# Expert output sums with 640 gathered and 1408 dense columns in place of 576 and 1472, and another place for the wait of a gathered sum

## The chip, the core and the metric

The kernel runs on one core of one Trainium2 chip. The metric is the device time of one execution in microseconds, the median of several. TensorE (PE) multiplies, VectorE (DVE) and ScalarE (ACT) work on tiles, GpSimd (POOL) issues the gathers here and SyncE (SP) issues the plain loads.

## What is computed

One decoder layer on 256 tokens of width 2048: a projection, two groups of recurrent heads, an output projection, and then a layer of 16384 single-neuron experts, with a final norm. The change touches only the second product of the expert layer. Cut to that:

```python
def peer_ffn(h, wq, keys, u_tab, v_tab):      # u_tab, v_tab: (16384, 2048)
    ...                                       # 128 experts and gates for each token
        u = jnp.take(u_tab, eb, axis=0)
        act = jax.nn.gelu(jnp.einsum("cd,ced->ce", xb, u))
        vv = jnp.take(v_tab, eb, axis=0)
        return jnp.einsum("ce,ced->cd", gb * act, vv)
...
x = x + peer_ffn(rms_norm(x, norm2_g), ...)
return rms_norm(x, normf_g)
```

## The kernel before

The work goes in stages: input projection with the recurrent heads, output projection, queries and top-16 choice, the product with all of `peer_u` (its result for all 16384 experts lies in `Zq`), a stage of gates (about 1355 to 1486 us of the profile) that turns `Zq` into a matrix of weights, token by expert, that is zero for experts not chosen, and then the V stage (1486 to 1993 us), which multiplies these weights with `peer_v`, and a tail with the final norm (to 2005 us).

**Two ways for V.** The 2048 columns of the output are split at `DD`. The first `DD` = 1472 columns are made densely on PE: for each of 128 expert rows i (a row is a block of 128 experts) SP loads `vraw` (128 partitions by 1472 columns, f32), ACT rounds it to `vhi`, DVE takes the rest as `vlo`, and PE adds three products (`vhi` with `a_hi`, `vlo` with `a_hi`, `vhi` with `a_lo`) into PSUM banks for both halves t of the tokens. The last `DS` = 576 columns are made sparsely: for each token half and each of its 128 picks POOL issues an indirect DMA that gathers one row piece per token into `got`, and DVE adds `got` times a weight to `sums`. That is 256 gathers and 256 sums, two for each expert row.

**Pieces.** Each expert row is loaded, rounded and subtracted in two pieces, k = 2i and 2i + 1: 1024 columns (two chunks of 512 for PE) and 448 columns (one chunk). `V_CUTS` holds the chunk limits; `dense` (L2257 and on) issues 2 x 3 x 3 = 18 matmuls for an expert row, 12 with 512 columns and 6 with 448. For the last expert row all 9 matmuls of t = 0 come before those of t = 1.

**What sets the order.** All queues are written out by hand. SP: `load_v(k)` (L494) waits until PE has finished piece k - 8 (4 buffers `vraw`), then issues the load. ACT: `v_hi(k)` (L948) waits for the load and for PE's piece k - 6 (3 buffers `vhi`). DVE: `v_lo(k)` (L1573) waits for ACT; behind each `v_lo(k)` from k = 6 on stands one `picked` (L1642), at every 40th piece two; every eighth piece has an `act_lo` too (L1634), which prepares the weights of four expert rows. PE: `dense` waits for `v_lo` of its piece. POOL: `gather(k)` (L628) waits until the sum k - 6 is done (6 buffers `got`); between gathers k = 128 and 223 it also issues eight loads of `xr` and four of `gf`.

A sum reads what the sum before it wrote (`sums[:, t]`), so it must not start until that one has landed. Before, `mark` does this: it puts an increment on the sum and a wait for it right behind it:

```python
def mark(ins, name, value):
    ins.then_inc(sem(name), 1)
    dve.wait_ge(sem(name), value)
```

so the wait holds whatever comes next on DVE, which mostly is a `v_lo`. The tail adds the dense sums to `xr` (L1675), squares, scales and sends rows out.

In the stage of gates, SP also issues the first eight pieces of `vraw` (one at every sixth step, from L522 on) between the small loads `oneJ` and `oneI` that PE and POOL need there.

Of the kernel before, what the change touches and what calls it, by code (L numbers as in the profile page):

```python
# [84 lines left out]
U_EXP = 50  # L85
U_FIRST = 65

DD = 1472
DS = D - DD
N_V_COLS = (PIECE, DD - PIECE)  # L90
V_CUTS = (0, 512, 1024, DD, D)
TOK4 = 4
LAST_TOKENS = (slice(0, 64), slice(64, SEQ))
N_TOK4 = SEQ // TOK4
# [3 lines left out]
N_GATHER = 6  # L98
V_RAWS, V_HIS = 4, 3
# [73 lines left out]
def hybrid_layer_kernel(nc, a, out):  # L173
    ctx = ExitStack()
    with ctx:
        sems = {}

        def sem(name):
            if name not in sems:
                sems[name] = ctx.enter_context(nc.semaphore(name))  # L180
            return sems[name]
# [4 lines left out]
        def at(name, shape, dt, offset):  # L186
            return nc.alloc_sbuf_tensor_at(name, shape, dt, offset=offset)
# [8 lines left out]
        raw_at = base[0]  # L196
# [19 lines left out]
        end = ARENA + 4 * ARENA_F  # L216
# [106 lines left out]
        wgt = at("wgt", [P, SEQ], F32, mshift_at + 1024)  # L323
        vraw = [at(f"vraw{i}", [P, DD], F32, raw_at + 4 * DD * i) for i in range(V_RAWS)]
        vlo = [at(f"vlo{i}", [P, DD], F32R, raw_at + 4 * DD * i) for i in range(V_RAWS)]
        vhi = [at(f"vhi{i}", [P, DD], F32R, raw_at + 24576 + 4 * DD * ((i + 2) % V_HIS))
               for i in range(V_HIS)]
        oneJ = [at(f"oneJ{i}", [P, TOK4, P], F32, raw_at + 43008 + 2048 * i) for i in range(N_ONEJ)]
        oneG = [at(f"oneG{i}", [P, TOK4, P], F32, raw_at + o)
                for i, o in enumerate((51200, 53248, 69632, 71680))]  # L330
# [6 lines left out]
                   for i in range(N_FIRST)]  # L337
        jcast = [at(f"jcast{i}", [P, BC_TOK, P], BF16,
                    raw_at + 4096 * (NR + slots[i // 2]) + 2048 * (i % 2)) for i in range(N_CAST)]
        a_hi = [at(f"a_hi{i}", [P, 4, SEQ], F32R, raw_at + 43008 + 4096 * i) for i in range(2)]  # L340
        a_lo = [at(f"a_lo{i}", [P, 4, SEQ], F32R, raw_at + 51200 + 4096 * i) for i in range(2)]
        got = [at(f"got{i}", [P, DS], F32, raw_at + 59392 + 4 * DS * ((i + 3) % N_GATHER))
               for i in range(N_GATHER)]
        wT = at("wT", [P, NT2, PICKS], F32, raw_at + 4 * DD * V_RAWS)
        assert 4 * DD * V_RAWS + 1024 <= 24576 and 24576 + 4 * DD * V_HIS <= 43008
        assert 59392 + 4 * DS * 3 >= 65536 + 768 and 59392 + 4 * DS * N_GATHER <= 73728
        madeJ = [ar(f"madeJ{i}", 30720 + 512 * i, [P, TOK4, P]) for i in range(3)]
        madeI = [ar(f"madeI{i}", 32256 + 256 * i, [P, TOK4, P], BF16) for i in range(2)]
        sums = ar("sums", 0, [P, NT2, DS])
        xr = ar("xr", 2048, [P, NT2, DD])  # L350
        gf = ar("gf", 6144, [P, D])
        xr_sq = ar("xr_sq", 8192, [P, 8, DS])
        xg = ar("xg", 13312, [P, PIECE])

        ps = ctx.enter_context(nc.psum_tensor("ps", [P, 8, 512], F32))
        jrow_dram = nc.dram_tensor("jrow_spill", (SEQ, PICKS), BF16, kind="Internal").ap()
# [106 lines left out]
        def _(sync):  # L463
            xv = a["x"].rearrange("o (t p) d -> p (o t) d", p=P)
            for t in range(NT2):
                for q in range(2):
                    part = slice(PIECE * q, PIECE * q + PIECE)
# [26 lines left out]
            def load_v(k):  # L494

                i, half = k // 2, k % 2
                cols_v = slice(PIECE * half, PIECE * half + N_V_COLS[half])
                sync.wait_ge(mm_done, 2 * T_V + max(k - 2 * V_RAWS + 1, 0))
                sync.dma_start(vraw[i % V_RAWS][:, cols_v], a["peer_v"][i, :, cols_v]).then_inc(
                    sem(f"v_in{k % (2 * V_RAWS)}"), 16)  # L500
# [40 lines left out]
            for k in range(2 * V_RAWS, 2 * N_V):  # L541
                load_v(k)
            outv = out.rearrange("o (t p) d -> p (o t) d", p=P)
            for q in range(6):
                t, j = q // 3, (3, 0, 2)[q % 3]
                if t and j == 0:
                    sync.wait_ge(sem("xg_done"), 1)
                else:
                    sync.wait_ge(sem(f"y_done{t}"), 2 if t and j == 2 else q % 3 + 1)
                first, end = V_CUTS[j], D if j == 3 else V_CUTS[j + 1] + (512 if j == 0 else 0)  # L550
                src = sums[:, t] if j == 3 else xg[:, :] if t and j == 0 else xr[:, t, first:end]
                sync.dma_start(outv[:, t, first:end], src).then_inc(sem("out_sent"), 16)
            sync.wait_ge(sem("out_sent"), 96)
# [113 lines left out]
        def _(act):  # L667
# [280 lines left out]
            def v_hi(k):  # L948

                i, half = k // 2, k % 2  # L950
                cols_v = slice(PIECE * half, PIECE * half + N_V_COLS[half])
                act.wait_ge(sem(f"v_in{k % (2 * V_RAWS)}"), 16 * (k // (2 * V_RAWS) + 1))
                act.wait_ge(mm_done, 2 * T_V + max(k - 2 * V_HIS + 1, 0))
                nc.scalar.activation(vhi[i % V_HIS][:, cols_v], vraw[i % V_RAWS][:, cols_v],  # L954
                                     ACT.Copy).then_inc(hi_done, 1)
# [102 lines left out]
        def _(dve):  # L1058
# [28 lines left out]
            def stt(o, i0, s, i1, op0, op1):  # L1087
                return V.scalar_tensor_tensor(out=o, in0=i0, scalar=s, in1=i1, op0=op0, op1=op1)  # L1088
# [126 lines left out]
            for g in range(GROUPS):  # L1215
# [96 lines left out]
                for c in range(4):  # L1312
# [302 lines left out]
            for s in range(N_TOK4 + S_LAG):  # L1615
# [678 lines left out]
```

## Time and profile before

| | us |
|---|---|
| median of 3 runs | 2005.94 (2005.63 to 2006.31) |
| the profiled execution, its own time | 2006.88 |
| its span, first to last instruction | 2005.0 |
| mean granted TensorE clock, share of full speed | 0.995 |
| DVE busy over the span | 1531.8 |
| ACT busy over the span | 975.6 |
| POOL busy over the span | 499.3 |
| HBM read and written | 430.24 MB and 29.43 MB |

The profiled execution took 1.9 us more than its span, and 0.94 us more than the median. PE here is the time in which matmuls are under way, PEld that of weight loads, which overlap it. The DMA share of a window is the mean busy share of the core's 16 DMA engines in it. A row of a timeline gives the start, the time it took, and in brackets how long the engine was idle before and what ended that; records of one kind that follow closely are merged (x2, x8), and the start of the next row is then the better measure of how long they took in the stream.

### The profile page before, as it was taken

To read this page: it belongs to the slowest core of one execution; us is meant where nothing else is said; L and a number is where in the kernel's file an instruction comes from. 1 tells how busy PE (TensorE), PEld (TensorE's weight loads), DVE (VectorE), ACT (ScalarE), POOL (GpSimd) and SP (SyncE) were. 2 spreads that over 40 slices of the span, in tenths; PEclk is the share of its full clock that TensorE was granted. 3 is DMA by queue.
4 is the path that set the end of the run, shared out by engine and by line. 5 is a ranking of instruction groups with operands and counts; after the bars stand their busy time and mean duration, and the time that the engine had idled before them with its cause. 6 is when DMAs were issued, how large, how long until landed. Compare 5 with 4: busy or idle time off the path is not lost.

```text
span 2005.0 us, 36029 instructions
## 1 busy us (share of the span) xinstructions
PE 1949.5 (97%) x14368; PEld 1732.9 (86%) x14368; DVE 1531.8 (76%) x2339; ACT 975.6 (49%) x1394; POOL 499.3 (25%) x511
## 2 busy tenths in 40 slices
PE   8999999999999999999999999999999999999997
PEld 7989888887899888888888888888888888888886
DVE  5557575667535999977878888758879989999997
ACT  5535454464544444444444444446665444444444
POOL 0000000000000000000012222105667666666663
PEclk9999999999999999999999999999999999999999
DMA  7523233245655666666578888768879999999996
GB/s 242 178 87 124 93 109 97 79 157 175 213 173 171 183 187 188 187 183 188 189 249 284 286 285 284 250 190 272 294 231 350 350 338 352 345 349 369 358 349 229
DMA packets 149607, 462.06 MB, mean 230 GB/s; under 512 B 19936, under 2 KB 45056, under 8 KB 148928
## 3 DMA queue, kind: packets, MB, share of 16 engines
q1 hardware_dynamic: 115760, 339.49, 52.3%
q0 software_dynamic: 33680, 120.26, 16.9%
q8 instruction: 115, 1.88, 0.4%
q14 instruction: 52, 0.43, 0.1%
HBM read 430.24 MB, written 29.43 MB: 229 GB/s over the span
## 4 chain that ended last, share of the span: by engine, by line
PE 87%; DVE 5%; DMA 3%; ACT 3%; issue 1%; SPq 0%; DVEq 0%; ACTq 0%
PE ps L1716 86%; DMA oneJ<-oneJ_spill 2%; DVE lo L1080 1%; DMA raw<-in_w_in 1%; ACT hi L677 1%; DMA raw<-in_w_out 0%; DVE hT L1088 0%; DVE xc L1088 0%; DVE TmTT L1292 0%; DVE L L1275 0%; DVE lr L1387 0%; PE ps L1876 0%; ACT x_sq L892 0%; DMA x_sb<-in_x 0%; ACT la L869 0%
## 5 line engine op out<-in xcount | busy, mean ns | idle before, releaser
L1716 PE MATMUL ps<-hT,hi 128*128 128x512 f32 (+1 forms) x3936 | 1075.1, 345 | 8.7 <-DVE rkv L1088 4.9
L1716 PE MATMUL ps<-hT,lo 128*128 128x256 f32 x2992 | 839.7, 281 | 0.0
L1716 PEld LDWEIGHTS ps<-hT,hi 128*128 128x128 f32 x3936 | 680.5, 190 | 108.6 <-DVE rkv L1088 6.0
L1080 DVE TENSOR_TENSOR lo<-raw,hi 128x1024 fp32r<-128x1024 f32 x406 | 492.6, 1224 | 227.7 <-ACT hi L677 221.4
L677 ACT ACTIVATE hi<-raw 128x1024 fp32r<-128x1024 f32 x406 | 424.4, 1059 | 441.0 <-DMA raw<-in_peer_u 371.8
L1716 PEld LDWEIGHTS ps<-hT,lo 128*128 128x128 f32 x2992 | 568.2, 190 | 0.0
L635 POOL DMA_INDIRECT got<-in_peer_v,row_ids x256 | 328.3, 1282 | 159.7 <-DVE sums L1088 98.6
L954 ACT ACTIVATE vhi<-vraw 128x1024 fp32r<-128x1024 f32 (+1 forms) x256 | 202.3, 816 | 271.0 <-DMA vraw<-in_peer_v 264.0
L1578 DVE TENSOR_TENSOR vlo<-vraw,vhi 128x1024 fp32r<-128x1024 f32 (+1 forms) x256 | 237.5, 929 | 43.0 <-ACT vhi L954 21.7
L1716 PE MATMUL ps<-vhi,a_hi 128*128 128x512 f32 (+1 forms) x768 | 251.7, 382 | 1.8 <-DVE a_lo L1634 1.6
L1716 PE MATMUL ps<-vlo,a_hi 128*128 128x512 f32 (+1 forms) x768 | 252.5, 383 | 0.0
L1716 PE MATMUL ps<-vhi,a_lo 128*128 128x512 f32 (+1 forms) x768 | 250.4, 381 | 0.0
L1088 DVE SCALAR_TENSOR_TENSOR sums<-got,wT,sums 128x576 f32<-128x576 f32 x256 | 207.7, 811 | 0.3
L1716 PEld LDWEIGHTS ps<-vlo,a_hi 128*128 128x128 f32 x768 | 144.2, 188 | 28.2
L1716 PEld LDWEIGHTS ps<-vhi,a_lo 128*128 128x128 f32 x768 | 144.2, 188 | 24.6
L1716 PEld LDWEIGHTS ps<-vhi,a_hi 128*128 128x128 f32 x768 | 144.1, 188 | 22.9 <-issue 2.3
L593 POOL DMA_DIRECT2D jrow_spill<-jrow x2 | 1.1, 543 | 452.4 <-DVE jrow L1512 452.4
L580 POOL DMA_DIRECT2D x<-in_x x1 | 0.7, 729 | 374.1 <-DVE yR_lo L1358 374.1
L597 POOL DMA_DIRECT2D oneJ_spill<-madeJ x64 | 34.6, 540 | 205.5 <-DVE madeJ L1554 205.5
L1425 DVE TENSOR_TENSOR Zq<-ps,Zq 128x256 f32<-128x256 f32 x129 | 78.6, 610 | 5.1 <-ACT Zq L922 5.1
L922 ACT ACTIVATE Zq<-ps 128x256 f32<-128x256 f32 x129 | 79.1, 613 | 5.1 <-PE ps L1716 4.8
L1716 PE MATMUL ps<-oneG,oneJ 128*128 128x128 f32 x512 | 69.0, 279 | 7.6 <-DMA oneJ<-oneJ_spill 7.4
(288 smaller groups left out, 1791.6 us busy)
## 6 DMA issues: line engine op xcount, KB each, us to landing
raw<-in_peer_u SPq DMA_DIRECT2D x256, 512.0 KB, 4.3
vraw<-in_peer_v SPq DMA_DIRECT2D x128, 512.0 KB
raw<-in_w_in SPq DMA_DIRECT2D x86, 512.0 KB, 3.6
vraw<-in_peer_v SPq DMA_DIRECT2D x128, 224.0 KB
raw<-in_w_out SPq DMA_DIRECT2D x32, 512.0 KB, 3.6
raw<-in_wq SPq DMA_DIRECT2D x32, 512.0 KB, 3.5
oneJ_spill<-madeJ POOLq DMA_DIRECT2D x64, 256.0 KB, 5.1
oneJ<-oneJ_spill SPq DMA_DIRECT2D x64, 256.0 KB, 4.7
```

The costliest lines, as they stand in the source:

```text
L580: pool.dma_start(x2[:, :, :], a["x"].rearrange("o (t p) d -> p (o t) d", p=P)).then_inc(sem("x2_in"), 16)
L593: pool.dma_start(jrow_dram[t * P:(t + 1) * P], jrow[:, t]).then_inc(sem("jrow_out"), 16)
L597: pool.dma_start(oneJ_dram[g], madeJ[g % 3][:, :, :].rearrange("p t j -> p (t j)")).then_inc(sem(f"oneJ_out{g % 3}"), 16)
L635: pool.indirect_dma_start(out=got[k % N_GATHER][:, :], out_offset=None, in_=v_rows, in_offset=bass.IndirectOffsetOnAxis(ap=row_ids[:, t, e ...
L677: nc.scalar.activation(hi[n % NR][:, :], raw[n % NR][:, :], ACT.Copy).then_inc(hi_done, 1)
L922: nc.scalar.activation(Zq[:, i // 4, part, i % 4], bank("tile", T_U + i)[:, part], ACT.Copy).then_inc(sem("z_in"), 1)
L954: nc.scalar.activation(vhi[i % V_HIS][:, cols_v], vraw[i % V_RAWS][:, cols_v], ACT.Copy).then_inc(hi_done, 1)
L1080: V.tensor_tensor(lo[n % NR][:, :], raw[n % NR][:, :], hi[n % NR][:, :].bitcast(F32), ALU.subtract).then_inc(lo_done, 1)
L1088: return V.scalar_tensor_tensor(out=o, in0=i0, scalar=s, in1=i1, op0=op0, op1=op1)
L1425: V.tensor_tensor(Zq[:, i // 4, part, i % 4], bank("tile", T_U + i)[:, lo_part], Zq[:, i // 4, part, i % 4], ALU.add).then_inc(freed("tile ...
L1578: V.tensor_tensor(vlo[i % V_RAWS][:, cols_v], vraw[i % V_RAWS][:, cols_v], vhi[i % V_HIS][:, cols_v].bitcast(F32), ALU.subtract).then_inc( ...
L1716: return nc.tensor.matmul(o, lhsT, rhs, start=start, stop=stop, skip_group_check=True)
```

## The change

Three things, in one edit:

- `DD` goes from 1472 to 1408, so 64 columns pass from the dense way to the gathered one: a gather moves 640 columns of a row (2560 B) instead of 576 (2304 B), and a sum works on 640. The counts stay at 256 each.
- The dense chunks become 480, 480 and 448 columns (`V_CUTS`), and the first piece of an expert row 960 columns instead of 1024 (`V_PIECE`); the second keeps 448. Offsets of `a_hi`, `a_lo` and `got` move with the sizes, and the parts of the tail that went by 512 and 1024 go by the cuts.
- `picked` no longer waits behind its sum. The wait for the sum before stands in front of the next sum.

```diff
-DD = 1472
+DD = 1408
 DS = D - DD
-N_V_COLS = (PIECE, DD - PIECE)
-V_CUTS = (0, 512, 1024, DD, D)
+V_CUTS = (0, 480, 960, DD, D)
+V_PIECE = V_CUTS[2]
+N_V_COLS = (V_PIECE, DD - V_PIECE)
...
-        a_hi = [at(f"a_hi{i}", [P, 4, SEQ], F32R, raw_at + 43008 + 4096 * i) for i in range(2)]
-        a_lo = [at(f"a_lo{i}", [P, 4, SEQ], F32R, raw_at + 51200 + 4096 * i) for i in range(2)]
-        got = [at(f"got{i}", [P, DS], F32, raw_at + 59392 + 4 * DS * ((i + 3) % N_GATHER))
+        a_hi = [at(f"a_hi{i}", [P, 4, SEQ], F32R, raw_at + 41984 + 4096 * i) for i in range(2)]
+        a_lo = [at(f"a_lo{i}", [P, 4, SEQ], F32R, raw_at + 50176 + 4096 * i) for i in range(2)]
+        got = [at(f"got{i}", [P, DS], F32, raw_at + 58368 + 4 * DS * ((i + 3) % N_GATHER))
...
-                cols_v = slice(PIECE * half, PIECE * half + N_V_COLS[half])
+                cols_v = slice(V_PIECE * half, V_PIECE * half + N_V_COLS[half])
...
             for j in range(2):
-                part = slice(512 * j, 512 * j + 512)
+                part = slice(V_CUTS[j], V_CUTS[j + 1])
...
                 t, e = k // PICKS, k % PICKS
                 dve.wait_ge(sem(f"got_in{k % N_GATHER}"), 16 * (k // N_GATHER + 1))
-                mark(stt(sums[:, t], got[k % N_GATHER][:, :], wT[:, t, e:e + 1], sums[:, t], ALU.mult,
-                         ALU.add), "picks_used", k + 1)
+                if k:
+                    dve.wait_ge(sem("picks_used"), k)
+                stt(sums[:, t], got[k % N_GATHER][:, :], wT[:, t, e:e + 1], sums[:, t], ALU.mult,
+                    ALU.add).then_inc(sem("picks_used"), 1)
...
-            scaled_out(0, xr[:, 0, 0:PIECE], slice(0, PIECE))
+            scaled_out(0, xr[:, 0, 0:V_PIECE], slice(0, V_PIECE))
```

The `cols_v` line changes alike in `load_v`, `v_hi` and `v_lo`, the `part` line in the tail of ACT and of DVE.

No instruction changes its place in a queue; a wait does, and sizes do. On DVE, in the middle of the V stage, the queue stood so before, with the semaphores that each instruction waits for in brackets (`picks_used` counts finished sums, `hi_done` pieces that ACT has rounded, `got_in` landed gathers):

```order
L1088 SCALAR_TENSOR_TENSOR sums<-got_206,wT,sums 128x576 [waits got_in4]
L1578 TENSOR_TENSOR vlo_161<-vraw_157,vhi_165 128x1024 [waits hi_done,picks_used]
L1088 SCALAR_TENSOR_TENSOR sums<-got_207,wT,sums 128x576 [waits got_in5]
L1578 TENSOR_TENSOR vlo_161<-vraw_157,vhi_165 128x448 [waits hi_done,picks_used]
L1634 TENSOR_TENSOR a_lo_201<-Zq,a_hi_199 128x1024 [waits ahi_done]
L1088 SCALAR_TENSOR_TENSOR sums<-got_202,wT,sums 128x576 [waits got_in0]
L1578 TENSOR_TENSOR vlo_162<-vraw_158,vhi_163 128x1024 [waits hi_done,picks_used]
L1088 SCALAR_TENSOR_TENSOR sums<-got_203,wT,sums 128x576 [waits got_in1]
```

and now:

```order
L1089 SCALAR_TENSOR_TENSOR sums<-got_206,wT,sums 128x640 [waits picks_used,got_in4]
L1579 TENSOR_TENSOR vlo_161<-vraw_157,vhi_165 128x960 [waits hi_done]
L1089 SCALAR_TENSOR_TENSOR sums<-got_207,wT,sums 128x640 [waits picks_used,got_in5]
L1579 TENSOR_TENSOR vlo_161<-vraw_157,vhi_165 128x448 [waits hi_done]
L1635 TENSOR_TENSOR a_lo_201<-Zq,a_hi_199 128x1024 [waits ahi_done]
L1089 SCALAR_TENSOR_TENSOR sums<-got_202,wT,sums 128x640 [waits picks_used,got_in0]
L1579 TENSOR_TENSOR vlo_162<-vraw_158,vhi_163 128x960 [waits hi_done]
L1089 SCALAR_TENSOR_TENSOR sums<-got_203,wT,sums 128x640 [waits picks_used,got_in1]
```

The wait for `picks_used` has gone from the `vlo` behind each sum to the next sum, which has a `vlo`, or the `a_lo`, between it and the sum it waits for.

The only place where two sums follow each other is the one at every 40th piece; before, on DVE:

```order
L1578 TENSOR_TENSOR vlo_161<-vraw_157,vhi_164 128x448 [waits hi_done,picks_used]
L1634 TENSOR_TENSOR a_lo_200<-Zq,a_hi_198 128x1024 [waits ahi_done]
L1088 SCALAR_TENSOR_TENSOR sums<-got_205,wT,sums 128x576 [waits got_in3]
L1088 SCALAR_TENSOR_TENSOR sums<-got_206,wT,sums 128x576 [waits got_in4,picks_used]
L1578 TENSOR_TENSOR vlo_162<-vraw_158,vhi_165 128x1024 [waits hi_done,picks_used]
```

and now:

```order
L1579 TENSOR_TENSOR vlo_161<-vraw_157,vhi_164 128x448 [waits hi_done]
L1635 TENSOR_TENSOR a_lo_200<-Zq,a_hi_198 128x1024 [waits ahi_done]
L1089 SCALAR_TENSOR_TENSOR sums<-got_205,wT,sums 128x640 [waits picks_used,got_in3]
L1089 SCALAR_TENSOR_TENSOR sums<-got_206,wT,sums 128x640 [waits picks_used,got_in4]
L1579 TENSOR_TENSOR vlo_162<-vraw_158,vhi_165 128x960 [waits hi_done]
```

There the second sum waits for the first in both, and the `vlo` behind it no longer does.

On PE an expert row (both token halves) stood so before, `x2` being two chunks in a row:

```order
L1716 MATMUL ps<-vhi_163,a_hi_198 128x512 x2
L1716 MATMUL ps<-vlo_159,a_hi_198 128x512 x2
L1716 MATMUL ps<-vhi_163,a_lo_200 128x512 x2
L1716 MATMUL ps<-vhi_163,a_hi_198 128x512 x2
L1716 MATMUL ps<-vlo_159,a_hi_198 128x512 x2
L1716 MATMUL ps<-vhi_163,a_lo_200 128x512 x2
L1716 MATMUL ps<-vhi_163,a_hi_198 128x448
L1716 MATMUL ps<-vlo_159,a_hi_198 128x448
L1716 MATMUL ps<-vhi_163,a_lo_200 128x448
L1716 MATMUL ps<-vhi_163,a_hi_198 128x448
L1716 MATMUL ps<-vlo_159,a_hi_198 128x448
L1716 MATMUL ps<-vhi_163,a_lo_200 128x448
```

and now:

```order
L1719 MATMUL ps<-vhi_163,a_hi_198 128x480 x2
L1719 MATMUL ps<-vlo_159,a_hi_198 128x480 x2
L1719 MATMUL ps<-vhi_163,a_lo_200 128x480 x2
L1719 MATMUL ps<-vhi_163,a_hi_198 128x480 x2
L1719 MATMUL ps<-vlo_159,a_hi_198 128x480 x2
L1719 MATMUL ps<-vhi_163,a_lo_200 128x480 x2
L1719 MATMUL ps<-vhi_163,a_hi_198 128x448
L1719 MATMUL ps<-vlo_159,a_hi_198 128x448
L1719 MATMUL ps<-vhi_163,a_lo_200 128x448
L1719 MATMUL ps<-vhi_163,a_hi_198 128x448
L1719 MATMUL ps<-vlo_159,a_hi_198 128x448
L1719 MATMUL ps<-vhi_163,a_lo_200 128x448
```

The twelve matmuls of 512 columns have 480 now, the order is the same.

## Rows read from the trace of the kernel before

**Rows 1.** The page: busy us of the engines; GB/s in 40 slices.
```profile
PE 1949.5 (97%) x14368; PEld 1732.9 (86%) x14368; DVE 1531.8 (76%) x2339; ACT 975.6 (49%) x1394; POOL 499.3 (25%) x511
...
GB/s 242 178 87 124 93 109 97 79 157 175 213 173 171 183 187 188 187 183 188 189 249 284 286 285 284 250 190 272 294 231 350 350 338 352 345 349 369 358 349 229
```

**Rows 2.** Chain of waits from 1300 us on: start us, us, what.
```profile
1498.75 492.47 PE ps L1716 x2241
...
1991.35 0.70 DVE xr L1675
```

**Rows 3.** Waits, 1500 to 1991 us: who <- whom, us in all, times, longest.
```profile
ACT vhi L954 <- DMA vraw<-in_peer_v: 256.5, 159, 4.7
POOL got L635 <- DVE sums L1088: 98.6, 64, 5.1
...
DVE vlo L1578 <- ACT vhi L954: 21.7, 33, 1.5
```

**Rows 4.** Waits of the SP queue, 1500 to 1991 us.
```profile
SPq L499 <- PE ps L1716: 356.7, 215, 2.8
```

**Rows 5.** Timeline of PE, one expert row: start us, us, what.
```profile
1700.47 0.62 PE L1716 MATMUL ps<-vhi,a_hi 128*128 128x512 f32 x2
...
1703.21 0.36 PE L1716 MATMUL ps<-vhi,a_hi 128*128 128x448 f32 x1
...
1704.42 0.62 PE L1716 MATMUL ps<-vhi,a_hi 128*128 128x512 f32 x2
```

**Rows 6.** Timeline of DVE, the same stretch.
```profile
1699.55 1.23 DVE L1578 TENSOR_TENSOR vlo<-vraw,vhi 128x1024 fp32r<-128x1024 f32 x1
1700.69 0.81 DVE L1088 SCALAR_TENSOR_TENSOR sums<-got,wT,sums 128x576 f32<-128x576 f32 x1
1701.54 0.62 DVE L1578 TENSOR_TENSOR vlo<-vraw,vhi 128x448 fp32r<-128x448 f32 x1
1702.08 0.81 DVE L1088 SCALAR_TENSOR_TENSOR sums<-got,wT,sums 128x576 f32<-128x576 f32 x1
```

**Rows 7.** Timeline of DVE, the tail: two sums with no wait between them.
```profile
1995.38 0.82 DVE L1088 SCALAR_TENSOR_TENSOR sums<-sums,scal,gf 128x576 f32<-128x576 f32 x1
1996.12 1.28 DVE L1088 SCALAR_TENSOR_TENSOR xr<-xr,scal,gf 128x1024 f32<-128x1024 f32 x1
```

**Rows 8.** Groups, 1500 to 1991 us: instructions, count, busy us, mean ns, idle before.
```profile
L635 POOL DMA_INDIRECT got<-in_peer_v,row_ids x250 | 320.2, 1281 | 156.7 <-DVE sums L1088 98.6 <-issue 58.1
...
L1634 DVE TENSOR_TENSOR a_lo<-Zq,a_hi 128x1024 fp32r<-128x1024 f32 x30 | 36.5, 1218 | 0.0
```

**Rows 9.** DMA view, 1495 to 1984 us: packets and bytes.
```profile
DMA packets 56811, 171.00 MB, mean 350 GB/s; under 512 B 8213, under 2 KB 24085, under 8 KB 56779
```

**Rows 10.** Windows: busy us by engine, granted clock, DMA share, GB/s.
```profile
1495.00:1535.00 40.00, 39.87 (x182) 33.79 (x181) 36.80 (x44) 17.63 (x22) 27.59 (x20) 1.00 0.99 354
...
1738.00:1778.00 40.00, 40.00 (x184) 34.19 (x183) 36.95 (x44) 18.79 (x24) 26.93 (x23) 1.00 1.00 369
1834.00:1874.00 40.00, 40.00 (x184) 34.23 (x183) 38.22 (x46) 19.40 (x24) 30.12 (x25) 1.00 1.00 368
1495.00:1984.00 489.00, 488.87 (x2226) 417.57 (x2225) 449.18 (x532) 223.43 (x277) 327.38 (x262) 1.00 0.97 350
```

**Rows 11.** Timeline of all engines, the end of the weight stream.
```profile
1983.20 1.67 ACT L954 ACTIVATE vhi<-vraw 128x1024 fp32r<-128x1024 f32 x2 [2.00 <-DMA vraw<-in_peer_v]
...
1986.35 0.62 DVE L1578 TENSOR_TENSOR vlo<-vraw,vhi 128x448 fp32r<-128x448 f32 x1
...
1989.06 0.83 PE L1716 MATMUL ps<-vhi,a_hi 128*128 128x512 f32 x3
```

**Rows 12.** Timeline of PE in the stage of gates.
```profile
1448.38 1.06 PE L1716 MATMUL ps<-Zq,oneJT 128*128 128x128 f32 x8
1451.97 2.08 PE L1716 MATMUL ps<-oneG,oneJ 128*128 128x128 f32 x8 [2.53 <-DMA oneJ<-oneJ_spill]
```

**Rows 13.** Windows in the stage of gates (columns as rows 10).
```profile
1451.90:1456.00 4.10, 4.03 (x21) 4.03 (x22) 2.02 (x4) 1.07 (x3) 2.04 (x2) 0.58 0.73 267
```

More of the change, by code:

```diff
@@ L339, in hybrid_layer_kernel @@
                     raw_at + 4096 * (NR + slots[i // 2]) + 2048 * (i % 2)) for i in range(N_CAST)]
-        a_hi = [at(f"a_hi{i}", [P, 4, SEQ], F32R, raw_at + 43008 + 4096 * i) for i in range(2)]
-        a_lo = [at(f"a_lo{i}", [P, 4, SEQ], F32R, raw_at + 51200 + 4096 * i) for i in range(2)]
-        got = [at(f"got{i}", [P, DS], F32, raw_at + 59392 + 4 * DS * ((i + 3) % N_GATHER))
+        a_hi = [at(f"a_hi{i}", [P, 4, SEQ], F32R, raw_at + 41984 + 4096 * i) for i in range(2)]
+        a_lo = [at(f"a_lo{i}", [P, 4, SEQ], F32R, raw_at + 50176 + 4096 * i) for i in range(2)]
+        got = [at(f"got{i}", [P, DS], F32, raw_at + 58368 + 4 * DS * ((i + 3) % N_GATHER))
                for i in range(N_GATHER)]
         wT = at("wT", [P, NT2, PICKS], F32, raw_at + 4 * DD * V_RAWS)
-        assert 4 * DD * V_RAWS + 1024 <= 24576 and 24576 + 4 * DD * V_HIS <= 43008
-        assert 59392 + 4 * DS * 3 >= 65536 + 768 and 59392 + 4 * DS * N_GATHER <= 73728
+        assert 4 * DD * V_RAWS + 1024 <= 24576 and 24576 + 4 * DD * V_HIS <= 41984
+        assert 58368 + 4 * DS * N_GATHER <= 73728
         madeJ = [ar(f"madeJ{i}", 30720 + 512 * i, [P, TOK4, P]) for i in range(3)]
@@ L352, in hybrid_layer_kernel @@
         xr_sq = ar("xr_sq", 8192, [P, 8, DS])
-        xg = ar("xg", 13312, [P, PIECE])
+        xg = ar("xg", 13312, [P, V_PIECE])
         ps = ctx.enter_context(nc.psum_tensor("ps", [P, 8, 512], F32))
@@ L549, in _ @@
                     sync.wait_ge(sem(f"y_done{t}"), 2 if t and j == 2 else q % 3 + 1)
-                first, end = V_CUTS[j], D if j == 3 else V_CUTS[j + 1] + (512 if j == 0 else 0)
+                first, end = V_CUTS[j], D if j == 3 else V_CUTS[j + 2 if j == 0 else j + 1]
                 src = sums[:, t] if j == 3 else xg[:, :] if t and j == 0 else xr[:, t, first:end]
@@ L950, in v_hi @@
                 i, half = k // 2, k % 2
-                cols_v = slice(PIECE * half, PIECE * half + N_V_COLS[half])
+                cols_v = slice(V_PIECE * half, V_PIECE * half + N_V_COLS[half])
                 act.wait_ge(sem(f"v_in{k % (2 * V_RAWS)}"), 16 * (k // (2 * V_RAWS) + 1))
@@ L1575, in v_lo @@
                 i, half = k // 2, k % 2
-                cols_v = slice(PIECE * half, PIECE * half + N_V_COLS[half])
+                cols_v = slice(V_PIECE * half, V_PIECE * half + N_V_COLS[half])
                 dve.wait_ge(hi_done, 2 * T_V + k + 1)
@@ L1698, in _ @@
             scaled_out(0, sums[:, 0], slice(DD, D))
-            scaled_out(0, xr[:, 0, 0:PIECE], slice(0, PIECE))
+            scaled_out(0, xr[:, 0, 0:V_PIECE], slice(0, V_PIECE))
             dve.wait_ge(sem("xr_done"), 6)
             for j in range(2):
-                part = slice(512 * j, 512 * j + 512)
+                part = slice(V_CUTS[j], V_CUTS[j + 1])
                 V.tensor_tensor(xg[:, part], xr[:, 1, part], gf[:, part], ALU.mult).then_inc(
@@ L1705, in _ @@
             row_sum(1)
-            scaled_out(0, xr[:, 0, PIECE:DD], slice(PIECE, DD))
+            scaled_out(0, xr[:, 0, V_PIECE:DD], slice(V_PIECE, DD))
             row_scale(1)
@@ L1709, in _ @@
             scaled_out(1, sums[:, 1], slice(DD, D))
-            scaled_out(1, xr[:, 1, PIECE:DD], slice(PIECE, DD))
+            scaled_out(1, xr[:, 1, V_PIECE:DD], slice(V_PIECE, DD))
         @block.tensor
```

## The prediction

> **What bounds the kernel now.** I read the page first, then the chain of waits, then the waits, and then single rows of the V stage. On the page PE is busy 97% of the span, and the transfers, low in the first half, are at 329 to 369 GB/s in every slice of the V stage [rows 1]. The reader should see two resources near their limit at once there. The chain of waits says which one sets the end: from 1498.75 us it is PE alone for 492.47 us, and the tail hangs on it from 1991.35 on [rows 2]. No wait of PE is in the list between 1500 and 1991 us; ACT waits 256.5 us for loads, POOL 98.6 us for sums to free a buffer, and DVE 21.7 us for ACT [rows 3]. The loads in turn are late only because SP waits for PE to free a buffer, 356.7 us in all [rows 4]. So PE paces everything, and the others idle around it.
>
> How near is the next limit? An expert row takes PE 1704.42 - 1700.47 = 3.95 us [rows 5]. In that time the DMA engines must move 128 x 1472 x 4 = 0.754 MB of dense columns and 2 x 128 x 576 x 4 = 0.590 MB of gathers, 1.344 MB or 340 GB/s. Over the whole stretch from 1495 to 1984 us it was 171.0 MB [rows 9] at 350 GB/s with the engines 97% busy [rows 10]. That leaves 3%.
>
> **PE.** Twelve matmuls of 512 columns take 1703.21 - 1700.47 = 2.74 us, 0.228 each; six of 448 take 1.21, 0.202 each [rows 5]. So 64 columns are worth 0.0267 us, and one with 480 should take 0.215. The change saves 12 x 0.0133 = 0.16 us on an expert row, which comes to 3.79, and 128 x 0.16 = 20.5 us in all. The clock was full in these windows [rows 10], so this is at 2.4 GHz. This is the whole gain if nothing else holds PE.
>
> **DVE.** Start to start, a `vlo` of 1024 columns takes 1.14 us, one of 448 0.54, and a sum 0.85 [rows 6]; an `act_lo` takes 1.22 every fourth expert row, 0.31 for one [rows 8]. Before: 1.14 + 0.54 + 2 x 0.85 + 0.31 = 3.69 of 3.95. The two pieces differ by 0.60 us for 576 columns, so 64 columns are 0.07. With the change, the first `vlo` takes 1.07 and a sum with its wait behind it would take 0.92: 3.76 of 3.79, no room left. What does moving the wait give? In the tail stands an operation of the same kind and size with no wait behind it, and the next starts 0.74 us after it instead of 0.85 [rows 7]. So a sum should take 0.81, and an expert row 1.07 + 0.54 + 1.62 + 0.31 = 3.54. Now the next sum is the instruction that waits, and since a `vlo` or `a_lo` stands between, it finds the count there already; only at the six double places it does not. What is queued behind a waiting sum is the next `vlo`, but got buffers are ready before they are needed: sums have no wait for gathers in the list [rows 3]. I cost the DVE part at nothing; its cover is PE's 3.79, and with the wait left behind the sum it would be as good as gone. The Trainium skill, page "VectorE: DVE Perf Modes", section "The DRAIN you can't avoid", says a semaphore after each operation costs nothing extra. By that rule the move gives nothing, and DVE stays at 3.76; the two spacings, 0.85 and 0.74, speak against it.
>
> **POOL and ACT.** A gather takes POOL 1.28 us and about 0.31 of issue behind it (58.1 over some 190), two make 3.2 of 3.79 [rows 8]. Should it grow with the size as the bytes do, by 11%, it would be 3.5. ACT has 64 columns less on an expert row and waits half its time [rows 3]. Both nothing.
>
> **Transfers, the term that decides.** The same 128 rows now are 0.721 MB dense and 0.655 MB gathered, 1.376 MB. In 3.79 us that is 363 GB/s, against 340. This is why I don't forecast the 20 us. I count the stretch 1495 to 1984 us, which ends about when the last load has landed: ACT's last pair starts at 1983.20, its second piece about a microsecond later [rows 11]. About 122 first pieces shrink by 128 x 64 x 4 = 32.8 kB each, -4.0 MB; 250 gathers grow by as much each, +8.2 MB [rows 8]. 171.0 + 4.2 = 175.2 MB. The time depends on a rate that the trace shows only in parts. From below: in the first 40 us, with the engines at 0.99, it was 354 GB/s. From above: in two other stretches of 40 us the engines were at 1.00 and moved 369 and 368 [rows 10]. I take the mean rate over the mean share, 350 / 0.97 = 361, as it rests on the longest stretch and lies in the middle. Then 175.2 / 0.361 = 485.3 us, and the last load lands at 1980.3, 3.7 us sooner than now.
>
> Behind that landing there is room that a late load uses up: the last `vlo` ends at 1986.97, and PE takes up the last expert row at 1989.06 [rows 11]. With transfers as the limit these 2.1 us go, a gain. The last expert row itself gives 0.2. Sum for the stage: 3.7 + 2.1 + 0.2 = 6.0.
>
> **Small terms.** In the stage of gates, four of the eight `vraw` loads that stand between the small loads shrink by 6%. One of the waits for `oneJ` took 2.53 us, and after it eight matmuls took 2.08 us instead of 1.06 [rows 12], with the granted clock at 0.58 on average, so mostly at 1.2 GHz [rows 13]. A shorter load may shorten this wait by 0.1, or spare the slow clock too: 0 to 2 us, I take 0.3. In the tail, two operations on `sums` grow by 0.07 us and the pieces of 1024 and 512 shrink by as much: nothing, 0.1 at most either way.
>
> Together 6.3 us. The profiled execution took 2006.88, so 2000.6; the median of the runs lies 0.94 below it, which makes **1999.6**.
>
> **The rivals.** *The full gain.* If saturated engines hold 369 GB/s, as in the best 40 us [rows 10], 175.2 MB need 474.8 us; the last load lands 14.2 us sooner, and with the 2.6 of the other terms it is 16.8: 1989.1. With more than that PE is the bound at 20.8: 1985.1. For it speaks that the short stretches come without a stall of PE; against it, that 369 was picked as the best of many, and stretches beside it are lower. Should the moved wait give nothing, the DVE would add its six double places and stay near 3.80, and this rival would lose a microsecond or two.
>
> *No change.* The transfers eat the gain. From 359.3 GB/s down to 353.5 the sum stays within 4.0 us of now. At 358, what the first 40 us give for full share (354 / 0.99), 489.4 us, landing 0.4 later than now, and 2.6 back: a gain of 2.2, 2003.7. The bytes that pass to the gathers are then paid by the same engines that PE had as its cover. The Trainium skill, page "DMA: Bandwidth & Descriptors", section Specifications, gives about 358 GB/s as the limit of one core at the memory. By that rule, with 358, the time is this 2003.7, and the trace agrees only over long stretches (350 over the whole), not over the two of 40 us at 368 and 369.
>
> *Slower: late loads.* If the saturated rate is that of the first 40 us, 354 [rows 10], 494.9 us are needed, the last load lands 5.9 later, and with 2.6 back it is 3.3 slower. PE then waits for `vlo` again and again; where one wait grows as long as the 2.53 us in the stage of gates, the clock drops as it did there, and eight matmuls lose 1.0, a stretch of 4 us nearly 2 [rows 12, 13]. One such near the end, where no cover is left, makes 5.1: 2011.0. It decides from about 354.8 GB/s down with such a drop, and 353.5 without. For it: the gathers are small pieces, and they gain share; against: only the first stretch was that slow.
>
> **How the numbers follow.** A difference of 0.2%, 4.0 us, is about what can be told from no change here. Forecast (359.3 to some 365 GB/s): 0.43. Full gain: 0.14. No change: 0.28. Slower: 0.15. Faster is the first two, 0.57. The range goes from 1988.5, which takes in the rival at 369, to 2010, which takes in 354 without a drop of the clock. Left out are the PE-bound end and the worst of the slower case, together under 2 in 10. The likeliest case by itself runs from 1994 to 2002.
>
> **What would show it.** Right: matmuls of 480 columns 0.215 apart; PE now has waits for `vlo` in the V stage, some 14 us in all; the DMA share is 0.99 or 1.00 from 1495 us to the end, at about 361 GB/s; a `vlo` starts 0.81 after a sum; the last `vlo` ends just before PE's last expert row. Wrong: a V stage without waits of PE (the full gain), a rate below 355, a spacing of 0.92 behind sums, waits of DVE for gathers, or the end of the stage set by POOL.

## The result

The changed kernel takes 1984.76 us (1982.95 to 1986.91, 4 runs), the kernel before 2005.79 us (2005.32 to 2006.31) beside it. The ratio is 0.9902, with an interval from 0.9888 to 0.9915: 21 us less, where 6.3 were forecast. The time lies under the range (1988.5 to 2010). It is the rival "the full gain", at its far end, where PE alone is the bound (1985.1), that came about.

The page of the changed kernel, busy times and rate in 40 slices, as [rows 1]:

```profile
PE 1930.5 (97%) x14368; PEld 1733.2 (87%) x14368; DVE 1523.4 (77%) x2339; ACT 970.6 (49%) x1394; POOL 501.0 (25%) x511
...
GB/s 239 182 87 128 87 118 97 66 152 177 203 179 169 184 189 185 187 185 186 189 227 282 287 285 286 277 189 233 307 235 363 365 369 368 363 385 377 377 374 256
```

Slices 31 to 39 lie in the V stage. Where 338 to 369 GB/s stood (the prediction's 329 is a misreading of this row), 363 to 385 stand now: in each of them the engines moved more than the 361 that I had taken for their limit. The chain of waits, as [rows 2]:

```profile
1485.62 485.87 PE ps L1719 x2295
...
1971.58 0.67 DVE xr L1678
```

PE alone makes the chain through the V stage, in one piece of 485.87 us, and the first DVE operation of the tail starts at 1971.58. Before, the V stage began with the piece

```profile
1486.51 12.11 PE ps L1716 x54
```

and ended at 1991.35 [rows 2]. So the stage is 504.8 us before and 486.0 after: 18.8 us. The rest of the 19.9 us between the two spans lies in the stage of gates, 3.0 us shorter (its matmuls waited 6.4 us for `oneJ` instead of 7.4, and the granted clock was 1.00 instead of 0.99), less 2.1 us that the stages ahead of it took longer, where the change has nothing.

The waits from 1500 us to the end of the V stage, as [rows 3]:

```profile
ACT vhi L955 <- DMA vraw<-in_peer_v: 231.9, 163, 3.5
POOL got L636 <- DVE sums L1089: 102.8, 151, 2.4
...
DVE vlo L1579 <- ACT vhi L955: 22.0, 35, 1.6
...
DVE sums L1089 <- DMA got<-in_peer_v,row_ids: 1.6, 2, 1.4
```

No row has PE as the one that waits. ACT still waits 231.9 us for loads and DVE 22.0 for ACT, as before: there is slack between them and PE. Two sums now wait for a gather, 1.6 us in all, which holds nothing else up.

The windows (columns as in [rows 10]):

```profile
1495.00:1535.00 40.00, 40.00 (x191) 35.49 (x191) 38.62 (x47) 19.24 (x25) 28.89 (x22) 1.00 1.01 381
...
1495.00:1965.00 470.00, 470.00 (x2222) 416.78 (x2222) 441.00 (x532) 219.30 (x278) 328.84 (x262) 1.00 1.00 372
```

Over the whole stretch 372 GB/s at a share of 1.00, 381 in the first 40 us, where the kernel before had 354 at 0.99. The DMA view of that stretch, as [rows 9]:

```profile
DMA packets 56748, 174.93 MB, mean 372 GB/s; under 512 B 8203, under 2 KB 24075, under 8 KB 56716
```

174.93 MB, as worked out (175.2). The bytes were right and the rate was not.

PE and DVE in the middle of the stage, as [rows 5, 6]:

```profile
1702.80 0.59 PE L1719 MATMUL ps<-vhi,a_hi 128*128 128x480 f32 x2
1703.23 0.59 PE L1719 MATMUL ps<-vlo,a_hi 128*128 128x480 f32 x2
...
1969.41 0.80 PE L1719 MATMUL ps<-vhi,a_hi 128*128 128x480 f32 x3
```

DVE:

```profile
1701.56 1.16 DVE L1579 TENSOR_TENSOR vlo<-vraw,vhi 128x960 fp32r<-128x960 f32 x1 [0.80 <-ACT vhi L955]
1702.63 0.88 DVE L1089 SCALAR_TENSOR_TENSOR sums<-got,wT,sums 128x640 f32<-128x640 f32 x1
1703.43 0.62 DVE L1579 TENSOR_TENSOR vlo<-vraw,vhi 128x448 fp32r<-128x448 f32 x1
```

Two matmuls of 480 columns take 0.43 us, 0.215 each, and a `vlo` starts 0.80 us behind a sum of 640 columns (forecast 0.215 and 0.81). The last expert row starts at 1969.41, 127 rows behind the first at 1485.62: 3.81 us each. Before, the same two starts are 1486.51 and 1989.06 [rows 11], 3.96 us each. So a row gives back 0.15 us, a little less than the 0.16 forecast.

### The profile page after: what moved, and what is told of

The parts are those of the page before. It is cut to its first block, busy times and chain, and to the rows that moved or that the text cites. A ratio compares the mean times of both kernels' runs of the same rounds, so it can differ in the third digit from the quotient of the medians.

```text
span 1985.1 us, 36029 instructions
## 1 busy us (share of the span) xinstructions
PE 1930.5 (97%) x14368; PEld 1733.2 (87%) x14368; DVE 1523.4 (77%) x2339; ACT 970.6 (49%) x1394; POOL 501.0 (25%) x511
## 4 chain that ended last, share of the span: by engine, by line
PE 87%; DVE 5%; DMA 3%; ACT 3%; issue 1%; DVEq 0%; SPq 0%; ACTq 0%
PE ps L1719 87%; DMA oneJ<-oneJ_spill 2%; DVE lo L1081 1%; ACT hi L678 1%; DMA raw<-in_w_in 1%; DMA raw<-in_w_out 0%; DVE hT L1089 0%; DVE xc L1089 0%; DVE TmTT L1293 0%; DVE L L1276 0%; DVE lr L1388 0%; PE ps L1879 0%; ACT x_sq L893 0%; DMA x_sb<-in_x 0%; DMA raw<-in_wq 0%
## 5 line engine op out<-in xcount | busy, mean ns | idle before, releaser
L955 ACT ACTIVATE vhi<-vraw 128x960 fp32r<-128x960 f32 (+1 forms) x256 | 197.7, 791 | 257.0 <-DMA vraw<-in_peer_v 239.7
L1579 DVE TENSOR_TENSOR vlo<-vraw,vhi 128x960 fp32r<-128x960 f32 (+1 forms) x256 | 227.4, 889 | 30.8 <-ACT vhi L955 22.0
L1719 PE MATMUL ps<-vhi,a_hi 128*128 128x480 f32 (+1 forms) x768 | 245.3, 374 | 1.6 <-DVE a_lo L1635 1.6
L1719 PE MATMUL ps<-vhi,a_lo 128*128 128x480 f32 (+1 forms) x768 | 245.4, 374 | 0.0
L1719 PE MATMUL ps<-vlo,a_hi 128*128 128x480 f32 (+1 forms) x768 | 245.1, 373 | 0.0
L1089 DVE SCALAR_TENSOR_TENSOR sums<-got,wT,sums 128x640 f32<-128x640 f32 x256 | 224.8, 878 | 2.2 <-DMA got<-in_peer_v,row_ids 1.6
```

The costliest lines, as they stand in the source:

```text
L1719: return nc.tensor.matmul(o, lhsT, rhs, start=start, stop=stop, skip_group_check=True)
```

## The experiments

For the V stage I give the time from the first to the last start of a `ps<-vhi,a_hi` matmul. It is 505.0 us before (1486.5 to 1991.5) and 486.1 after (1485.6 to 1971.7). It says more than the whole time where a difference is small, since the stage of gates before it varies by itself: its waits and the granted clock differ from one execution to the next, and the kernel before, timed beside the first four kernels below, spread from 2000.45 to 2007.54 us. The kernels were timed in three sets, on more than one chip; where two times come from different sets, I go by the V stage.

### The wait undone, and the wait alone

```diff
-                if k:
-                    dve.wait_ge(sem("picks_used"), k)
-                stt(sums[:, t], got[k % N_GATHER][:, :], wT[:, t, e:e + 1], sums[:, t], ALU.mult,
-                    ALU.add).then_inc(sem("picks_used"), 1)
+                mark(stt(sums[:, t], got[k % N_GATHER][:, :], wT[:, t, e:e + 1], sums[:, t], ALU.mult,
+                         ALU.add), "picks_used", k + 1)
```

> The changed kernel with one part undone: the wait for a gathered sum stands behind the sum again (1408 dense and 640 gathered columns, chunks of 480, 480 and 448 stay). Theory 1 (PE alone paces the V stage, the sizes give the whole gain): DVE then needs 3.76 us for an expert row, with the double places 3.80, and PE 3.80, so the time stays within 2 us of the changed kernel, 1984 to 1987 us, and a vlo starts 0.92 us behind a sum instead of 0.81. Theory 2 (the room that the moved wait makes on DVE is what let the gain through): DVE becomes the bound, waits of PE for vlo appear, 1988 us or more.

It took 1985.53 us (ratio 0.9895, 0.9879 to 0.9912), a V stage of 486.4 us. The kernel before with the opposite edit:

> The kernel before with the moved wait alone (1472 dense and 576 gathered columns stay). Theory 1: PE does not wait for DVE in the V stage, so nothing changes, 2005 to 2006.5 us, though a vlo starts 0.74 us behind a sum instead of 0.85. Theory 2: some of the gain is here, 2003 us or less.

2005.27 us (ratio 1.0, 0.999 to 1.001; 11 runs, one of them, the profiled one, at 2014.01, which it lost ahead of the V stage), V stage 504.6. Theory 2 falls with both: at these sizes the wait is worth nothing in time, and the sizes are worth all that the V stage gained. On DVE it is worth what the rows said. With 576 columns and the wait moved, a `vlo` starts 0.73 us behind a sum, where it was 0.85 [rows 6]:

```profile
1702.71 0.81 DVE L1088 SCALAR_TENSOR_TENSOR sums<-got,wT,sums 128x576 f32<-128x576 f32 x1
1703.44 0.61 DVE L1578 TENSOR_TENSOR vlo<-vraw,vhi 128x448 fp32r<-128x448 f32 x1
```

The timeline of the changed kernel with the wait behind the sum:

```profile
1699.98 0.88 DVE L1089 SCALAR_TENSOR_TENSOR sums<-got,wT,sums 128x640 f32<-128x640 f32 x1
1700.89 0.63 DVE L1579 TENSOR_TENSOR vlo<-vraw,vhi 128x448 fp32r<-128x448 f32 x1
1701.43 0.88 DVE L1089 SCALAR_TENSOR_TENSOR sums<-got,wT,sums 128x640 f32<-128x640 f32 x1
1702.35 1.16 DVE L1579 TENSOR_TENSOR vlo<-vraw,vhi 128x960 fp32r<-128x960 f32 x1
```

0.91 us from a sum to the next `vlo`, and 0.92, against 0.80. DVE is busy 389 of 400 us here:

```profile
1500.00:1900.00 400.00, 400.00 (x1891) 354.89 (x1890) 389.29 (x453) 187.81 (x237) 300.26 (x227) 1.00 1.00 373
```

and 375 in the changed kernel:

```profile
1500.00:1900.00 400.00, 400.00 (x1892) 354.79 (x1891) 375.43 (x454) 186.74 (x236) 282.56 (x227) 1.00 1.00 374
```

It is just enough for PE's 3.81 us, so nothing shows in the end.

### The chunks

```diff
-V_CUTS = (0, 480, 960, DD, D)
+V_CUTS = (0, 512, 1024, DD, D)
```

> The changed kernel with the same split of columns (1408 dense, 640 gathered) and the chunks 512, 512 and 384 instead of 480, 480 and 448, so the first piece of an expert row is 1024 columns again (4096 B of each partition) and the second 384. PE: 12 x 0.228 + 6 x 0.175 = 3.79 us for an expert row, as now. Theory 1 (PE paces by the number of columns): within 2 us of the changed kernel. Theory 3 (the smaller first piece is what made the transfers faster: its packets of 3840 B took 0.0426 ns per byte, those of 4096 B before 0.0444): the rate of the V stage falls from 372 towards 361 GB/s, PE waits for loads, 1990 to 2000 us.

1990.69 us (ratio 0.9929, 0.9906 to 0.9952), V stage 488.7. That is 5 us over the changed kernel in time, measured in another set of runs, but 2.6 in the V stage. So I ran it again, with the changed kernel on the same chip.

> The kernel with chunks of 512, 512 and 384 once more, beside the changed kernel on one chip. In its first profile the V stage took 490.31 us against 487.75, with PE idle in neither, so its matmuls of 384 columns took longer than 0.175 us. If that is so again: 2 to 3 us over the changed kernel. If the 1990.7 us of its first timing is a cost of the chunks: 5 us or more over it.

> The changed kernel once more, as a measure on the same chip for the three beside it. No theory is tested: 1983 to 1987 us.

1988.18 us (1985.73 to 1990.51) against 1985.73 (1981.96 to 1986.58), and V stages of 489.3 and 487.7, the latter with 3.4 us at half clock at its start, which made its first expert row 5.46 us long instead of 3.81. The PE timeline of the kernel with 512, 512 and 384:

```profile
1700.93 0.33 PE L1719 MATMUL ps<-vhi,a_hi 128*128 128x384 f32 x1
...
1702.00 0.63 PE L1719 MATMUL ps<-vhi,a_hi 128*128 128x512 f32 x2
...
1704.76 0.33 PE L1719 MATMUL ps<-vhi,a_hi 128*128 128x384 f32 x1
```

Six matmuls of 384 columns take 1.07 us, 0.178 each, where 0.175 was expected from the slope. The twelve of 512 take 2.76, 0.230 each, where it was 0.228 in the kernel before. So an expert row takes 3.83 us instead of 3.81, and the chunks 480, 480 and 448 are better by 2 to 3 us in the V stage. Between the whole times of the two kernels on one chip the intervals overlap, and the 5 us of the first timing did not come again. Why a matmul of 512 columns takes 0.002 us more here is not shown. Theory 3 falls: the transfers moved 369 GB/s with pieces of 4096 B again, without a wait of PE for data (the first profile of this kernel):

```profile
1495.00:1965.00 470.00, 469.98 (x2212) 407.47 (x2211) 439.42 (x529) 219.10 (x279) 319.75 (x261) 1.00 0.99 369
```

### What the transfers can do

Here the step that failed is measured by itself. Four kernels whose V stage keeps all loads and gathers while PE and DVE have much less to do (the last edit below, where a gather starts in the row, stands in the third of them alone):

```diff
                 for w, lhsT, s, e in (...):
+                    if lhsT is al and i < N_V - 1:
+                        continue
...
-                stt(sums[:, t], got[k % N_GATHER][:, :], wT[:, t, e:e + 1], sums[:, t], ALU.mult,
+                stt(sums[:, t, 0:64], got[k % N_GATHER][:, 0:64], wT[:, t, e:e + 1], sums[:, t, 0:64], ALU.mult,
...
-                    element_offset=DD).then_inc(
+                    element_offset=1408).then_inc(
```

> The kernel before with PE and DVE unburdened in the V stage, so that the transfers alone can pace it: the product of vhi with a_lo is left out for all expert rows but the last, and each sum works on 64 of its 576 columns (both leave out part of the second expert product). All loads and gathers stay, 1.344 MB for an expert row. PE would need 2.64 us for one, DVE about 2.5, POOL 3.2. Theory S (the long packets of the kernel before come from queues that had run empty; its 359 GB/s per busy time is no limit): the rate rises to 385 GB/s or more, the share over 1.00, the V stage takes 172.6 MB / 0.39 = 440 us instead of 507, the kernel about 1940 us. Theory L (the layout sets the rate: pieces of 4096 B and gathers of 2304 B that start 5888 B into a row run at 359 at most): about 359 GB/s, V stage 480 us, the kernel about 1980 us.

> The changed kernel with the same parts left out (1.376 MB for an expert row, pieces of 3840 and 1792 B, gathers of 2560 B that start 5632 B into a row). Theory S: the same rate as the kernel before with the cut, 385 GB/s or more, V stage about 450 us. Theory L: 372 to 381 GB/s as in the changed kernel, and over 10 GB/s more than the kernel before with the cut.

> The kernel before with the same parts left out, and its gathers start at column 1408 (5632 B into a row, a multiple of 512) instead of 1472 (5888 B); they still move 576 columns, so the wrong columns are summed. Theory L in its alignment form: the gathers run faster than in the same kernel with 1472, 5 GB/s or more in the V stage. Theory S: no difference beyond 3 GB/s.

> The kernel with 1344 dense and 704 gathered columns, with the same parts left out (1.409 MB for an expert row, pieces of 3584 and 1792 B, gathers of 2816 B). It shows how far that kernel is from the limit of the transfers, which gave 390 GB/s with PE idle 3.5 us. Theory S: some 395 to 405 GB/s, near that of the other three. Theory L: 390 GB/s, well over the kernel before with the cut.

The windows view from 1500 to 1900 us, first of the kernel before, uncut:

```profile
1500.00:1900.00 400.00, 400.00 (x1823) 341.93 (x1822) 370.33 (x439) 184.43 (x229) 273.15 (x221) 1.00 0.98 352
```

The kernel before with the cut:

```profile
1500.00:1900.00 400.00, 327.66 (x1376) 249.69 (x1374) 292.59 (x491) 210.27 (x257) 286.39 (x245) 1.00 1.03 394
```

The changed kernel with the cut:

```profile
1500.00:1900.00 400.00, 317.86 (x1343) 250.35 (x1342) 271.65 (x479) 199.88 (x252) 257.25 (x240) 0.97 1.03 394
```

The kernel before with the cut and gathers from column 1408:

```profile
1500.00:1900.00 400.00, 328.53 (x1366) 252.16 (x1365) 290.24 (x487) 208.14 (x255) 286.92 (x245) 0.99 1.03 391
```

1344 dense columns with the cut:

```profile
1500.00:1900.00 400.00, 300.59 (x1307) 249.17 (x1306) 258.59 (x468) 190.32 (x247) 251.64 (x234) 0.96 1.03 395
```

With the layout of the kernel before, the same 16 engines moved 394 GB/s, not 359 to 361. The changed layout gives 394, the shifted gathers 391 and the smallest pieces 395. Theory L falls in both forms: neither the size of the pieces nor where in a row a gather starts changes the rate by more than 1%. Both starts are multiples of 256 B; the kernel with 1376 dense columns below has one that is not (5504 B), and reached 396.

Is 394 a limit? The rate in 40 slices of 10 us, from 1500 to 1900 us, first of the kernel before, then of its cut form:

```profile
GB/s 368 333 366 352 333 380 330 362 372 314 348 335 329 364 311 339 378 329 363 354 324 339 350 331 397 356 353 377 329 357 343 334 389 359 365 363 363 373 332 370
...
GB/s 385 391 397 396 397 396 396 397 397 392 395 398 396 396 397 395 396 391 392 396 394 396 394 398 392 389 393 394 397 396 368 387 395 395 397 396 393 396 389 397
```

Uncut it goes up and down between 311 and 397. Cut it stays between 385 and 398 but for one slice of 368, and the other three cut kernels are much the same, with a few more dips. That speaks for a limit of the transfers. But a load still waited there until PE had freed its buffer (SP waited 321.8 of the 400 us for that), so whether more loads under way would move more is not tested. I take about 394 for what this stream can keep up; an expert row of the changed kernel asks for 361 (1.376 MB in 3.81 us). The cut kernels took 1948.26, 1953.62, 1955.92 and 1965.56 us (one run each), in the order of their bytes but for the third; V stages 451.7, 458.2, 454.5 and 470.1. The first is 12 us longer than the 440 worked out from bytes and rate alone, the second 8 longer than 450. PE was idle 18 to 25% from 1500 to 1900 us, waiting for `vlo` behind ACT behind the loads. The waits of the first, 1500 to 1915 us:

```profile
ACT vhi L954 <- DMA vraw<-in_peer_v: 191.0, 169, 3.0
...
DVE vlo L1578 <- ACT vhi L954: 98.7, 95, 3.1
...
PE ps L1716 <- DVE vlo L1578: 73.3, 90, 2.5
```

These are the waits that I had forecast for the changed kernel. At the start of its V stage PE waited 4.19 us in one piece, and in the 5 us behind that the granted clock was 0.50, 1.2 GHz (timeline of PE, then windows):

```profile
1493.70 1.19 PE L1716 MATMUL ps<-vhi,a_hi 128*128 128x512 f32 x2 [4.19 <-DVE vlo L1578]
...
1493.70:1498.70 5.00, 5.00 (x12) 4.09 (x13) 3.12 (x7) 2.31 (x3) 3.77 (x4) 0.50 1.04 406
```

Why did 350 GB/s come with a share of 0.97? The DMA view of the same window (queue, packets, MB, share of 16 engines) in the kernel before:

```profile
q1 hardware_dynamic: 29306, 76.61, 53.2%
q0 software_dynamic: 17404, 63.68, 44.4%
```

and in its cut form:

```profile
q1 hardware_dynamic: 32841, 86.02, 56.3%
q0 software_dynamic: 19447, 71.21, 46.9%
```

Over 400 us the queue with the loads took 16 engines for 2.78 us per MB before and 2.62 in the cut kernel, the queue with the gathers 2.79 and 2.63, with packets of the same sizes. In the mean of this window packets of 4096 B took 182 ns before and 167 in the cut kernel, those of 4608 B (two gathered pieces) 204 and 192, those of 1792 B 77 in both. So the longer packets took less of an engine's time when there was more to do, and the shares of the queues add up to more than 1. That busy time holds some waiting which goes away under load, and that the queues had run empty between bursts, as theory S has it, fits this; neither was looked at by itself.

### One and two steps further

```diff
-DD = 1408
+DD = 1344
...
-V_CUTS = (0, 480, 960, DD, D)
+V_CUTS = (0, 448, 896, DD, D)
```

(and the places of `vhi`, `a_hi`, `a_lo`, `got` and `xg`, so that they fit)

> One step further: 1344 dense columns in three chunks of 448 and 704 gathered ones, wait in front of the next sum (buffers moved to fit). PE 18 x 0.202 = 3.63 us for an expert row, DVE 1.00 + 0.54 + 2 x 0.88 + 0.31 = 3.61, transfers 1.409 MB, 388 GB/s to keep up. If PE still paces: 20.5 us less, 1964 us. If the 372 GB/s of the changed kernel is the limit of the engines: 3.79 us for an expert row and no gain, 1982 to 1985 us. If they reach the 381 GB/s of its best 40 us: about 1973 us.

**1970.98 us** (1970.53 to 1977.22; ratio 0.9834, 0.9813 to 0.9854), V stage 475.1: 14 us less than the changed kernel in time, 11 in the V stage. The 1964 of "PE still paces" isn't reached, the 1982 of a limit at 372 is far off, and the 1973 worked out for 381 GB/s is nearest. Its window:

```profile
1500.00:1900.00 400.00, 396.46 (x1936) 362.40 (x1935) 387.36 (x461) 187.99 (x242) 306.68 (x232) 1.00 1.02 390
```

It moved 390 GB/s at a share of 1.02, and now PE waits for `vlo` here and there. The V stage is 10 us longer than the 465 that 18 matmuls of 0.202 us in a row make. PE was idle for 3.6 of them, the granted clock was 0.66 in the first 5 us, and the matmuls stood 0.205 us apart in the mean of the stage; what lengthened those is not shown. PE, DVE (387 of 400 us) and the transfers (390 of 394) all stand within 4% of full use, so I expect no gain from another step of this size; none was run.

The same kernel with the wait behind the sum:

> The kernel with 1344 dense and 704 gathered columns, but with the wait behind the sum as in the kernel before. DVE then needs 1.00 + 0.54 + 2 x 0.99 + 0.31 = 3.83 us for an expert row, 490 us for 128, where PE needs 3.63 and the transfers at 394 GB/s 3.58. If the spacing of 0.85 against 0.74 is real, DVE is the bound: a V stage of about 490 us instead of 477, 1982 to 1986 us against 1971. If the semaphore costs nothing: 1971 us, no difference.

1987.87 us (1985.17 to 1990.03; ratio 0.9922, 0.9902 to 0.9943), 2 us over the range given, but V stage 490.9, where 490 was worked out from 0.99 us for a sum. Its waits:

```profile
POOL got L636 <- DVE sums L1089: 99.8, 213, 2.1
PEld ps L1717 <- issue: 24.9, 30, 1.7
PE ps L1717 <- DVE vlo L1579: 13.9, 23, 1.4
```

Its DVE timeline:

```profile
1701.48 0.94 DVE L1089 SCALAR_TENSOR_TENSOR sums<-got,wT,sums 128x704 f32<-128x704 f32 x1
1702.46 0.62 DVE L1579 TENSOR_TENSOR vlo<-vraw,vhi 128x448 fp32r<-128x448 f32 x1
```

Its window:

```profile
1500.00:1950.00 450.00, 436.93 (x2111) 393.84 (x2110) 441.82 (x504) 207.13 (x266) 342.78 (x252) 1.00 1.01 377
```

And the DVE timeline of the kernel with the wait in front:

```profile
1700.76 0.95 DVE L1089 SCALAR_TENSOR_TENSOR sums<-got,wT,sums 128x704 f32<-128x704 f32 x1
1701.62 0.62 DVE L1579 TENSOR_TENSOR vlo<-vraw,vhi 128x448 fp32r<-128x448 f32 x1
```

0.98 against 0.86 us. DVE is the bound, PE waits 23 times for `vlo`, the rate falls to 377 GB/s, and 16 us of the V stage are lost (17 of the time, in different sets of runs). So the moved wait, worth nothing with 640 columns, is the condition for the step to 704. Between the two:

> Between the two: 1376 dense columns in chunks of 464, 464 and 448, 672 gathered, wait in front. PE 12 x 0.209 + 6 x 0.202 = 3.72 us for an expert row, 476 us in all; transfers 1.393 MB, 374 GB/s, well under 394; DVE 1.04 + 0.54 + 2 x 0.84 + 0.31 = 3.57. With PE as the bound and 394 GB/s as the limit of the transfers: a V stage of 477 us without waits of PE, 1974 us. With a limit of 373 to 381: 1980 us or more.

1974.90 us (1971.3 to 1976.78; ratio 0.9851, 0.983 to 0.9872), V stage 476.7, PE waiting once, 0.3 us: as worked out. Its window:

```profile
1500.00:1945.00 445.00, 444.67 (x2146) 402.58 (x2146) 428.84 (x514) 211.28 (x270) 332.82 (x257) 1.00 1.01 385
...
1710.00:1720.00 10.00, 10.00 (x50) 9.06 (x49) 8.34 (x11) 5.52 (x7) 5.34 (x5) 1.00 1.03 418
...
1750.00:1850.00 100.00, 100.00 (x484) 90.62 (x483) 95.96 (x116) 47.76 (x60) 74.63 (x63) 1.00 1.02 396
```

385 GB/s over 445 us with no loss, 396 over 100 us with PE never idle, and 418 over one stretch of 10. So 394 is no ceiling for short stretches.

## Why the prediction was wrong

**Right:** PE sets the end before, with no wait. Matmuls of 480 columns take 0.215 us in the rows above. An expert row takes 3.81 us instead of 3.79, as over the whole stage they stand 0.216 apart and those of 448 columns 0.203, and so 18.8 of the 20.5 us came in the V stage. DVE's count was right to 0.01 us for a sum with and without the wait behind it, the bytes to 0.3 MB. POOL and ACT did not matter. The stage of gates gave its small share, but as it varies by itself, in the profiles here by several us, no run assigns it to the change. That the whole came to 21.0 us, within 0.3 of the 20.8 of the rival, is in part luck: 2 us of it lie outside the V stage.

**The step that failed** is the rate in the term of the transfers: "I take the mean rate over the mean share, 350 / 0.97 = 361". The rate that this stream reaches is 394, measured with the layout of the kernel before. With 394, the 175.2 MB need 445 us, where PE needs 486, and the term is nothing; the sum is then 20.5 + 0.3 = 20.8, 1985.1 us, as the rival had it. All that hung on this, the 14 us of waits of PE, a landing just ahead of the last expert row, and the likeliest case with 0.43, falls with it.

What misled was a division that looks harmless. The kernel before needed 340 GB/s and got 350 because PE asked for no more; a measured rate of a stream that something else paces is what was asked for, not what can be had. Its busy share of 0.97 seemed to say that 3% were left, while about 13% were. The stretches at 368 and 369 stood in the rows [rows 10]: there the loads of `xr` and `gf` came on top, PE did not wait at all, and what can be kept up for 40 us without a stall is a bound from below for the limit, not the best of a scatter. I read it as a bound from above. Of the 40 slices of 10 us above, from the same trace, 16 lay over 361, up to 397. With the bounds turned round, at least 369 and unknown above, the full gain would have been the likeliest case.

**No change** at 358 GB/s: fell. The Trainium skill, page "DMA: Bandwidth & Descriptors", section Specifications, gives a limit of about 358 GB/s for one core, as half of what a stack of memory has for two. It doesn't hold in these runs, where the kernel has one core: 372 over 470 us in the changed kernel, 394 over 400 us in the cut ones. **Slower, late loads:** fell; no wait of PE at all in the V stage. In the cut kernels, where such waits are real, the mean granted clock from 1500 to 1900 us lay between 0.96 and 1.00, and it was 0.50 behind the wait of 4.19 us above, so that part of the mechanism exists once PE starves. **Moved wait:** the Trainium skill, page "VectorE: DVE Perf Modes", section "The DRAIN you can't avoid", says that a semaphore after each operation costs nothing extra. Here the sum raises its semaphore in both forms, and what moves is the wait for it: that costs 0.11 to 0.12 us each time another instruction of the engine stands right behind it, and 16 us of the V stage once DVE is the bound.

## What to carry to other kernels

A busy share near 1 on a stream that another engine paces says neither that the stream is at its limit nor how far off it is. Take the fastest stretch in which nobody waited as what is surely there, and to know the limit, take the pacing work out and let the stream run. A wait on an engine's own last result belongs in front of the instruction that reads it: it may be free today, and be what the next step stands on.

## What the hardware showed beyond what I expected

Sixteen DMA engines moved 391 to 395 GB/s from HBM over 400 us with rows of 1792 to 4096 B and gathered pieces of 2304 to 2816 B, whatever the mix, at a share of 1.03. Busy time per byte fell by about 6% from a rate of 352 to one of 394. And a DVE instruction that waits for its own engine's last result starts 0.11 to 0.12 us later than one that doesn't, at 576, 640 and 704 columns alike.
